# Expert weights of up and down in 1 MB halves, with neighbouring rows in one partition

## The chip, the cores and the metric

The kernel runs on one core of a Trainium2 chip. The metric is the device time of one execution in microseconds (us). The kernel before takes 813.57 us (median of three runs, 813.0 to 815.25).

## The reference

One encoder layer over two sequences, 512 and 256 tokens of width 1024, all in float32: LayerNorm, two attention groups on one input projection, an output projection, LayerNorm, and a mixture of 16 experts (each token goes to the two best of one group of four), then a last LayerNorm. The part that matters here is the mixture:

```python
h = jax.nn.silu(xt @ w_gate[e]) * (xt @ w_up[e])
y = y + gates[:, e:e + 1] * (h @ w_down[e])
```

`w_gate[e]` and `w_up[e]` are 1024 x 512, `w_down[e]` is 512 x 1024; each is 2 MB, so an expert is 6 MB.

## The kernel before

The first 460 us or so (LayerNorm, projections, attention, router) are left as they are. After that the mixture works through tiles: a tile is up to 128 token rows of one expert. The 16 experts need 17 tiles here, and each tile loads its 6 MB of weights anew. The loop is written by hand for each engine; each engine runs its own list in order, and semaphores tie the lists together.

**SP** issues the weight loads (function `load`, L2076 to L2081). Each matrix X (G for gate, U for up, D for down) of a tile comes as four units of 512 KB into the buffers `raw[X][0..3]`, one tile deep: unit i of tile t is issued when the units i of the tile before have been used up (semaphore `s_lo[X]`). In one turn of the loop SP goes through U of the next tile, G of the tile after it, D of the next tile.

**ACT** and **DVE** split each unit for a matmul in two parts: ACT rounds it to `wh_[X][i]` (L2229), after it has landed (`s_raw[X][i]`), and DVE stores the rest, `wl_[X][i]` (L2300). Only when DVE is done with it is the `raw` buffer free.

**POOL** gathers the 128 token rows of the next tile into `xg` with an indirect DMA, and adds the finished rows of a tile to DRAM with another.

**PE** turns the gathered rows (`turn_x`, L2128: eight 128 x 128 transposes of `xg`), multiplies by gate and up (L2143 to L2145, three matmuls for each of eight chunks), turns the hidden rows (`turn_h`, L2152: four transposes of `hid`) and multiplies by down (L2164 to L2166). In a transpose the piece of `xg` or `hid` is the stationary operand: PE loads it with a weight load (PEld in the profile), and the identity streams past.

Which rows of a weight lie in one partition decides which columns of `xg` a chunk takes. A unit of G or U holds 256 rows, two neighbouring rows (4 KB) in each partition, so chunk c takes every second column of `xg`. A unit of D holds 128 rows, one in each partition, so chunk c takes 128 neighbouring columns of `hid`.

Of the kernel before, what the change touches and what calls it, by code (L numbers as in the profile page):

```python
# [27 lines left out]
P = 128  # L28
# [17 lines left out]
FF = 512  # L46
# [14 lines left out]
def encoder_trunk(nc, x_prompt, x_sample, ln0_g, ln0_b, w_in, g_q, g_kv, w_uq, w_ukv, lam_q1, lam_k1,  # L61
# [34 lines left out]
    ident = small("ident", [P, P])  # L96
# [286 lines left out]
    ax = [at(f"ax{i}", (38, 198)[i], [P, D]) for i in range(2)]  # L383
    x1T = at("x1T", 202, [P, KD, P])

    raw = {X: [at(f"raw{X}{i}", 78 + 16 * n + 4 * i, [P, 2 * FF]) for i in range(4)] for n, X in enumerate("GUD")}

    raw_g2 = [at(f"rawG2{i}", (70, 194, 198, 202)[i], [P, 2 * FF]) for i in range(4)]

# [87 lines left out]
    s_lo = {X: sem(f"e{X}_low") for X in "GUD"}  # L477
    s_raw = {X: [sem(f"raw{X}{i}_landed") for i in range(4)] for X in "GUD"}

    def unit_src(X, e, i):  # L480

        if X == "D":
            return w_down[0, bass.ds(e, 1), i * P:(i + 1) * P, :].rearrange("a p n -> p (a n)")
        w = w_gate if X == "G" else w_up
        return w[0, bass.ds(e, 1), 2 * i * P:(2 * i + 2) * P, :].rearrange("a (p c) n -> p (a c n)", c=2)

    def unit_dst(X, i, t=0):
        return raw_of(X, t, i)[:]
# [1155 lines left out]
    with nc.Block() as block:  # L1644

        @block.sync
        def _(sp):
            front_sync(sp)
            sp.wait_ge(s_pv, 3 * NT)
            for i in range(3):  # L1650
                sp.dma_start(unit_dst("G", i), unit_src("G", 0, i)).then_inc(s_raw["G"][i], 16)
            sp.wait_ge(s_o, 12)
            sp.dma_start(ln1g_sb[:], bcast(ln1_g[0], D)).then_inc(s_ln1w, 16)
            sp.dma_start(ln1b_sb[:], bcast(ln1_b[0], D)).then_inc(s_ln1w, 16)
            sp.wait_ge(s_pv, DT)
            sp.dma_start(wr_sb[:], w_router.rearrange("(c p) n -> p c n", p=P)).then_inc(s_rt, 16)
            sp.dma_start(br_sb[:], bcast(b_router, NE)).then_inc(s_rt, 16)
            for X in "UD":
                for i in range(4):
                    sp.dma_start(unit_dst(X, i), unit_src(X, 0, i)).then_inc(s_raw[X][i], 16)  # L1660
            sp.wait_ge(s_zrow, 1)
            sp.dma_start(x1_rows[TOK:TOK + 1, :], ax[1][0:1, :]).then_inc(s_zst, 16)
            sp.dma_start(acc_rows[TOK:TOK + 1, :], ax[1][0:1, :]).then_inc(s_zst, 16)
            for t in range(NT):
                if t == NT - 1:
                    sp.wait_ge(s_o, 24)
                    sp.dma_start(unit_dst("G", 3), unit_src("G", 0, 3)).then_inc(s_raw["G"][3], 16)
                sp.wait_ge(s_x1, t + 1)
                sp.dma_start(x1_rows[t * P:(t + 1) * P, :], res[:, t, :]).then_inc(s_x1st, 16)
                sp.wait_ge(s_ax, t + 1)  # L1670
                sp.dma_start(acc_rows[t * P:(t + 1) * P, :], ax[t % 2][:]).then_inc(s_stored[t % 2], 16)
            sp.wait_ge(s_zst, 32)
            for i in range(2):
                sp.wait_ge(s_stored[i], 16 * (NT // 2))
            sp.wait_ge(s_x1st, 16 * NT)

            for i in range(4):
                sp.wait_ge(s_lo["G"], i + 1)
                sp.dma_start(unit_dst("G", i), unit_src("G", 1, i)).then_inc(s_raw["G"][i], 16)


            sp.wait_ge(s_o, 24)
            sp.wait_ge(s_log, NT)
            for i in range(4):
                sp.wait_ge(s_raw["G"][i], 32)
                sp.dma_start(unit_dst("G", i, 2), unit_src("G", 2, i)).then_inc(s_raw["G"][i], 16)

        @block.tensor
        def _(pe):
# [60 lines left out]
        @block.scalar  # L1750
        def _(act):
            front_act(act)

            def high0(X, units):

                for i in units:
                    act.wait_ge(s_raw[X][i], 16)
# [314 lines left out]
    with nc.Block() as block:  # L2072

        @block.sync
        def _(sp):
            def load(X, t):  # L2076
                e = sp.value_load(tile_expert[0:1, bass.ds(t, 1)], min_val=0, max_val=NE - 1)
                for i in range(4):

                    sp.wait_ge(s_lo[X], 4 * t + i - 3)  # L2080
                    sp.dma_start(unit_dst(X, i), unit_src(X, e, i)).then_inc(s_raw[X][i], 16)  # L2081


            for X in "UD":
                for i in range(4):
                    sp.wait_ge(s_lo[X], i + 1)
                    sp.dma_start(unit_dst(X, i), unit_src(X, 1, i)).then_inc(s_raw[X][i], 16)
            load("U", 2)
            for i in range(4):

                sp.wait_ge(s_raw["G"][i], 48)
                sp.wait_ge(s_lo["G"], 4 + i + 1)
                sp.dma_start(unit_dst("G", i), unit_src("G", 3, i)).then_inc(s_raw["G"][i], 16)
# [12 lines left out]
            sp.wait_ge(s_scatter, 16 * count - 16)  # L2106
            for t in range(NT):
                sp.dma_start(res[:, t, :], acc_rows[t * P:(t + 1) * P, :]).then_inc(s_acc[t], 16)
            for t in range(NT):
                sp.wait_ge(s_yr, t + 1)  # L2110
                dst = y_prompt[0, t * P:(t + 1) * P, :] if t < NT_P else y_sample[0, (t - NT_P) * P:(t - NT_P + 1) * P, :]
                sp.dma_start(dst, res[:, t, :]).then_inc(s_out, 16)
            sp.wait_ge(s_out, 16 * NT)

        @block.tensor
        def _(pe):
            def xg_chunk(c):

                return xg[:].rearrange("p (i m j) -> p i j m", i=4, j=2)[:, c // 2, c % 2, :]

            def turn_x(t):

# [8 lines left out]
            def inner(X, t, units):  # L2131

                out = psum["GU".index(X)][:]
                for i in units:
# [10 lines left out]
                        last = nc.tensor.matmul(out, xgT_h[:, c, :], wl_[X][i][:, cs], start=False, stop=(c == KD - 1))  # L2145
                    last.then_inc(s_used[X], 1)

            def turn_h(t):
                wait(pe, s_hid, t + 1)
                wait(pe, s_hl, t)  # L2150
                for j in range(4):
                    last = nc.tensor.transpose(psum[6][:, j * P:(j + 1) * P], hid[:, j * P:(j + 1) * P], ident[:])  # L2152
                last.then_inc(s_ht, 1)

            def down(t):
# [67 lines left out]
        def _(act):  # L2223
            def high(X, t, units=range(4)):
                for i in units:
                    wait(act, s_raw[X][i], 16 * t + 16)

                    wait(act, s_used[X], used0[X] + 4 * t + i - 3)
                    nc.scalar.activation(wh_[X][i][:], raw_of(X, t, i)[:], ACT.Copy).then_inc(s_hi[X], 1)  # L2229
# [266 lines left out]
```

## Time and profile before

| what | value |
|---|---|
| median of the runs | 813.57 us |
| profiled execution | 813.27 us |
| its span, first to last instruction | 811.5 us |
| PE busy | 736.1 us (91%) |
| DVE busy | 584.5 us (72%) |
| ACT busy | 482.3 us (59%) |
| share of the chain that ended last: PE, DMA | 18%, 15% |

The shares are means over the whole span; the mixture, from about 464 us on, has its own limits and is read from its own stretch. A time in a row below counts from the start of the span. "granted clock" or PEclk is the clock that TensorE was granted, as a share of 2.4 GHz. The chain of waits follows the work that ended last back from the end of the program.

### The profile page before, as it was taken

To read this page: it belongs to the slowest core of one execution; us is meant where nothing else is said; L and a number is where in the kernel's file an instruction comes from. 1 tells how busy PE (TensorE), PEld (TensorE's weight loads), DVE (VectorE), ACT (ScalarE), POOL (GpSimd) and SP (SyncE) were. 2 spreads that over 40 slices of the span, in tenths; PEclk is the share of its full clock that TensorE was granted. 3 is DMA by queue.
4 is the path that set the end of the run, shared out by engine and by line. 5 is a ranking of instruction groups with operands and counts; after the bars stand their busy time and mean duration, and the time that the engine had idled before them with its cause. 6 is when DMAs were issued, how large, how long until landed. Compare 5 with 4: busy or idle time off the path is not lost. (4 is left out here: it accounts for less than half of the span.)

```text
span 811.5 us, 12644 instructions
## 1 busy us (share of the span) xinstructions
PE 736.1 (91%) x3799; PEld 607.6 (75%) x3799; DVE 584.5 (72%) x975; ACT 482.3 (59%) x874; POOL 265.6 (33%) x293
## 2 busy tenths in 40 slices
PE   3999989998899789999998299999999999999985
PEld 3898878877788577767787177888887777777862
DVE  6974355555545676777675879999988888888757
ACT  3344345555544656676035347888878778888635
POOL 3133266655654233334421024222222222222111
PEclk9999999999999969999996589999999999999998
DMA  9724220222025673212734649999999999999763
GB/s 342 250 87 149 98 78 2 79 65 65 2 65 179 211 308 117 70 49 78 290 124 174 241 138 363 384 375 390 396 379 385 376 375 365 388 384 375 284 207 155
DMA packets 71484, 179.35 MB, mean 221 GB/s; under 512 B 11687, under 2 KB 28071, under 8 KB 71444
## 3 DMA queue, kind: packets, MB, share of 16 engines
q1 hardware_dynamic: 66692, 166.34, 54.4%
q0 software_dynamic: 4752, 12.51, 6.2%
q8 instruction: 22, 0.36, 0.2%
q14 instruction: 18, 0.15, 0.1%
HBM read 153.20 MB, written 30.42 MB: 226 GB/s over the span
## 5 line engine op out<-in xcount | busy, mean ns | idle before, releaser
L2300 DVE TENSOR_TENSOR eDl<-rawD,eDh 128x1024 fp32r<-128x1024 f32 x68 | 80.3, 1221 | 12.0 <-ACT eDh L2229 11.8
L1265 POOL TENSOR_SCALAR me<-me,mrec 128x512 f32<-128x512 f32 (+1 forms) x48 | 64.9, 1354 | 55.4 <-DVE mrec L1444 55.4
L2300 DVE TENSOR_TENSOR eUl<-rawU,eUh 128x1024 fp32r<-128x1024 f32 x68 | 78.8, 1220 | 4.5 <-ACT eUh L2229 2.3
L2300 DVE TENSOR_TENSOR eGl<-rawG,eGh 128x1024 fp32r<-128x1024 f32 x64 | 75.6, 1221 | 7.0 <-ACT eGh L2229 6.7
L2424 POOL DMA_INDIRECT acc_rows<-yg,idx_s x16 | 29.7, 1859 | 134.1 <-ACT yg L2254 134.1
L2229 ACT ACTIVATE eGh<-rawG 128x1024 fp32r<-128x1024 f32 x64 | 65.5, 1058 | 6.9 <-DMA rawG<-in_w_gate 5.8
L1071 ACT ACTIVATE pT_h<-bank 128x512 fp32r<-128x512 f32 (+1 forms) x48 | 25.2, 526 | 73.9 <-PE bank L781 73.9
L1450 DVE TENSOR_TENSOR pT_l<-bank,pT_h 128x512 fp32r<-128x512 f32 (+1 forms) x48 | 28.9, 602 | 50.2 <-ACT pT_h L1071 50.2
L2229 ACT ACTIVATE eDh<-rawD 128x1024 fp32r<-128x1024 f32 x64 | 64.0, 1056 | 0.0
L2143 PE MATMUL bank<-eGh,xgT_h 128*128 128x512 f32 x136 | 56.8, 417 | 7.6 <-DVE xgT_l L2305 6.5
L2229 ACT ACTIVATE eUh<-rawU 128x1024 fp32r<-128x1024 f32 x64 | 62.7, 1052 | 0.0
L2143 PE MATMUL bank<-eUh,xgT_h 128*128 128x512 f32 x136 | 54.6, 401 | 0.0
L2145 PE MATMUL bank<-eGl,xgT_h 128*128 128x512 f32 x136 | 54.1, 398 | 0.0
L2144 PE MATMUL bank<-eGh,xgT_l 128*128 128x512 f32 x136 | 53.8, 395 | 0.0
L2145 PE MATMUL bank<-eUl,xgT_h 128*128 128x512 f32 x136 | 53.2, 391 | 0.0
L2144 PE MATMUL bank<-eUh,xgT_l 128*128 128x512 f32 x136 | 52.9, 389 | 0.0
L2166 PE MATMUL bank<-eDl,hT_h 128*128 128x512 f32 x128 | 49.9, 390 | 0.0
L2164 PE MATMUL bank<-eDh,hT_h 128*128 128x512 f32 x128 | 49.8, 389 | 0.0
L2165 PE MATMUL bank<-eDh,hT_l 128*128 128x512 f32 x128 | 49.8, 389 | 0.0
L646 PE MATMUL bank<-xT_h,wb_h 128*128 128x256 f32 (+1 forms) x128 | 44.9, 351 | 3.9 <-DVE q_raw L1431 2.4
L646 PE MATMUL bank<-xT_h,wb_l 128*128 128x256 f32 (+1 forms) x128 | 43.8, 342 | 0.0
L2235 ACT ACTIVATE xgT_h<-bank 128x512 fp32r<-128x512 f32 x34 | 20.3, 596 | 39.5 <-PE bank L2145 26.9
(343 smaller groups left out, 2184.7 us busy)
## 6 DMA issues: line engine op xcount, KB each, us to landing
rawG<-in_w_gate SPq DMA_DIRECT2D x68, 512.0 KB, 14.9
rawU<-in_w_up SPq DMA_DIRECT2D x68, 512.0 KB, 11.7
rawD<-in_w_down SPq DMA_DIRECT2D x68, 512.0 KB, 13.1
wb_raw<-in_w_in SPq DMA_DIRECT2D x8, 512.0 KB, 4.7
wo_raw<-in_w_o SPq DMA_DIRECT2D x8, 512.0 KB, 7.5
xln_rows<-res SPq DMA_DIRECT2D x6, 512.0 KB, 3.9
dqk_high<-st_h SPq DMA_DIRECT2D x8, 384.0 KB, 2.3
dqk_low<-st_l SPq DMA_DIRECT2D x8, 384.0 KB, 3.3
```

The source lines that it names most:

```text
L646: last = nc.tensor.matmul(out, pairs[i][0], pairs[i][1], start=(i == 0), stop=(i == n - 1))
L1265: nc.gpsimd.tensor_scalar(e, e, mrec[:, g % NSB:g % NSB + 1], None, ALU.mult).then_inc(m_p, 1)
L1450: nc.vector.tensor_tensor(pT_l[x][:, :, qs], psum[2 + g % 2][:, 0:n].rearrange("p (j q) -> p j q", q=P), f32(pT_h[x][:, :, qs]), ALU.subtr ...
L2143: nc.tensor.matmul(out, xgT_h[:, c, :], wh_[X][i][:, cs], start=(c == 0), stop=False)
L2144: nc.tensor.matmul(out, xgT_l[:, c, :], wh_[X][i][:, cs], start=False, stop=False)
L2145: last = nc.tensor.matmul(out, xgT_h[:, c, :], wl_[X][i][:, cs], start=False, stop=(c == KD - 1))
L2164: nc.tensor.matmul(out, hT_h[:, cs], wh_["D"][c][:, ns], start=(c == 0), stop=False)
L2165: nc.tensor.matmul(out, hT_l[:, cs], wh_["D"][c][:, ns], start=False, stop=False)
L2166: last = nc.tensor.matmul(out, hT_h[:, cs], wl_["D"][c][:, ns], start=False, stop=(c == 3))
L2229: nc.scalar.activation(wh_[X][i][:], raw_of(X, t, i)[:], ACT.Copy).then_inc(s_hi[X], 1)
L2300: nc.vector.tensor_tensor(wl_[X][i][:], raw_of(X, t, i)[:], f32(wh_[X][i][:]), ALU.subtract).then_inc(s_lo[X], 1)
L2424: pool.indirect_dma_start(out=acc_rows, out_offset=bass.IndirectOffsetOnAxis(ap=idx_s[:, 0:1], axis=0), in_=yg[:], in_offset=None, bounds_ ...
```

## The change

The units of U and D are loaded in pairs. A pair is one DMA of 1 MB: 512 rows of U with four neighbouring rows (8 KB) in each partition, or 256 rows of D with two neighbouring rows (8 KB). The buffers of a pair are one tile; the four `raw` units are views into it, so that ACT and DVE work on the same units as before. G stays in units of 512 KB, but its rows take the same order as those of U: of the four rows that belong to a partition, unit 0 takes the first two and unit 1 the last two, so that it reads 4 KB out of every 8 KB. The chunks follow: chunk c of `xg` takes every fourth column (before every second), chunk c of `hid` every second (before neighbouring ones).

```diff
+    raw_pair = {X: [at(f"pair{X}{h}", 78 + 16 * n + 8 * h, [P, 4 * FF]) for h in range(2)] for n, X in enumerate("GUD") if n}
+    raw = {X: [raw_pair[X][i // 2][:, i % 2 * 2 * FF:(i % 2 + 1) * 2 * FF] for i in range(4)] for X in "UD"}
...
+    def pair_src(X, e, h):
         if X == "D":
-            return w_down[0, bass.ds(e, 1), i * P:(i + 1) * P, :].rearrange("a p n -> p (a n)")
+            return w_down[0, bass.ds(e, 1), 2 * h * P:(2 * h + 2) * P, :].rearrange("a (p c) n -> p (a c n)", c=2)
+        return w_up[0, bass.ds(e, 1), 4 * h * P:(4 * h + 4) * P, :].rearrange("a (p c) n -> p (a c n)", c=4)
+    def gate_src(e, i):
+        rows = w_gate[0, bass.ds(e, 1), 4 * (i // 2) * P:(4 * (i // 2) + 4) * P, :].rearrange("a (p c) n -> p a c n", c=4)
+        return rows[:, :, 2 * (i % 2):2 * (i % 2) + 2, :].rearrange("p a c n -> p (a c n)")
+    def landed(X, i):
+        return s_raw[X][i if X == "G" else i // 2]
...
-                for i in range(4):
+                for i in range(4) if X == "G" else (1, 3):
                     sp.wait_ge(s_lo[X], 4 * t + i - 3)
-                    sp.dma_start(unit_dst(X, i), unit_src(X, e, i)).then_inc(s_raw[X][i], 16)
+                    if X == "G":
+                        sp.dma_start(unit_dst(X, i), gate_src(e, i)).then_inc(s_raw[X][i], 16)
+                    else:
+                        sp.dma_start(raw_pair[X][i // 2][:], pair_src(X, e, i // 2)).then_inc(s_raw[X][i // 2], 16)
...
             def xg_chunk(c):
-                return xg[:].rearrange("p (i m j) -> p i j m", i=4, j=2)[:, c // 2, c % 2, :]
+                return xg[:].rearrange("p (h m k) -> p h k m", h=2, k=4)[:, c // 4, c % 4, :]
...
+            def hid_chunk(c):
+                return hid[:].rearrange("p (h m k) -> p h k m", h=2, k=2)[:, c // 2, c % 2, :]
...
-                    last = nc.tensor.transpose(psum[6][:, j * P:(j + 1) * P], hid[:, j * P:(j + 1) * P], ident[:])
+                    last = nc.tensor.transpose(psum[6][:, j * P:(j + 1) * P], hid_chunk(j), ident[:])
...
             def high(X, t, units=range(4)):
                 for i in units:
-                    wait(act, s_raw[X][i], 16 * t + 16)
+                    wait(act, landed(X, i), 16 * t + 16)
```

On SP the loads of U in the loop stand like this in the kernel before. An ISA row with a wait stands for the wait of the DMA behind it; `eU_low` counts the units of U that DVE has finished.

```order
L2080 REGISTER_ALU
L2081 ISA [waits eU_low]
L2081 DMA rawU0_203<-in_w_up 128x1024
L2080 REGISTER_ALU
L2081 ISA [waits eU_low]
L2081 DMA rawU1_204<-in_w_up 128x1024
L2080 REGISTER_ALU
L2081 ISA [waits eU_low]
L2081 DMA rawU2_205<-in_w_up 128x1024
L2081 ISA [waits eU_low]
L2081 DMA rawU3_206<-in_w_up 128x1024
```

And the same place after the change:

```order
L2089 REGISTER_ALU
L2093 ISA [waits eU_low]
L2093 DMA pairU0_199<-in_w_up 128x2048
L2093 ISA [waits eU_low]
L2093 DMA pairU1_200<-in_w_up 128x2048
```

Four loads with four waits became two loads with two waits, each for the second unit of its pair. D changes in the same way, and G keeps its four loads.

On ACT the rounding of U in the first turn of the loop stands like this before (`rawU0_landed` is the semaphore of the load of unit 0):

```order
L2229 ACTIVATE eUh0_215<-rawU0_203 128x1024 [waits eU_used,rawU0_landed]
L2229 ACTIVATE eUh1_216<-rawU1_204 128x1024 [waits eU_used,rawU1_landed]
L2229 ACTIVATE eUh2_217<-rawU2_205 128x1024 [waits eU_used,rawU2_landed]
L2229 ACTIVATE eUh3_218<-rawU3_206 128x1024 [waits eU_used,rawU3_landed]
L2241 ACTIVATE gsil_6322<-bank0 128x512 [waits hidden,eG_used]
```

And after the change:

```order
L2245 ACTIVATE eUh0_211<-pairU0_199 128x1024 [waits eU_used,rawU0_landed]
L2245 ACTIVATE eUh1_212<-pairU0_199 128x1024 [waits eU_used,rawU0_landed]
L2245 ACTIVATE eUh2_213<-pairU1_200 128x1024 [waits eU_used,rawU1_landed]
L2245 ACTIVATE eUh3_214<-pairU1_200 128x1024 [waits eU_used,rawU1_landed]
L2257 ACTIVATE gsil_6314<-bank0 128x512 [waits hidden,eG_used]
```

The first unit of a pair now waits for the whole pair. No instruction of PE, DVE or POOL moves; PE's twelve transposes for each tile read their stationary operand at another step.

## Rows read from the trace of the kernel before

**Rows 1.** Busy time of each engine by stretch, with granted clock and DMA share.

```profile
core 0: us, PE busy (x) PEld busy (x) DVE busy (x) ACT busy (x) POOL busy (x), PEclk, DMA share, GB/s
480.00:500.00 20.00, 18.95 (x89) 15.29 (x87) 19.30 (x22) 12.91 (x16) 6.83 (x5) 1.00 0.72 249
560.00:580.00 20.00, 20.00 (x95) 16.71 (x94) 18.44 (x19) 17.00 (x22) 5.22 (x6) 1.00 1.03 393
660.00:680.00 20.00, 19.30 (x90) 15.73 (x89) 17.72 (x17) 16.37 (x21) 4.93 (x5) 1.00 1.01 375
```

**Rows 2.** Chain of waits, transposes on it: start us, us, what.

```profile
474.57 0.95 PE bank L2128 x8
...
513.03 1.22 PE bank L2128 x8
...
540.27 0.44 PE bank L2152 x4
...
548.90 0.95 PE bank L2128 x8
...
566.71 0.94 PE bank L2128 x8
...
751.81 0.94 PE bank L2128 x8
```

**Rows 3.** Chain of waits, 605 to 734 us.

```profile
605.05 16.07 DMA rawG<-in_w_gate
...
642.38 16.31 DMA rawG<-in_w_gate
658.71 1.07 ACT eGh L2229
659.81 1.24 DVE eGl L2300
661.19 16.26 DMA rawG<-in_w_gate
...
717.54 16.30 DMA rawG<-in_w_gate
```

**Rows 4.** Weight loads of transposes, both lines, 530 to 590 us (ns min/median/max).

```profile
L2128 PEld LDWEIGHTS bank<-ident,xg x32: 195/209/209, 530.7 to 585.0; 128*128 128x128 f32 x32
...
L2152 PEld LDWEIGHTS bank<-ident,hid x12: 138/139/140, 539.9 to 575.9; 128*128 128x128 f32 x12
```

**Rows 5.** Weight loads of transposes at half clock, and those stretches' clock.

```profile
L1700 PEld LDWEIGHTS bank<-ident,res x11: 224/230/370, 433.8 to 440.3; 128*128 128x128 f32 x11
...
L2128 PEld LDWEIGHTS bank<-ident,xg x8: 197/226/226, 464.3 to 465.6; 128*128 128x128 f32 x8
...
434.00:441.00 7.00, 6.25 (x29) 5.45 (x27) 3.50 (x3) 5.59 (x8) 0.00 (x0) 0.50 0.76 246
...
464.00:466.60 2.60, 1.96 (x8) 1.58 (x8) 1.79 (x2) 0.92 (x2) 0.18 (x1) 0.50 0.08 28
```

**Rows 6.** DMA of 605 to 735 us, then of 93 to 102 us.

```profile
DMA packets 14023, 49.35 MB, mean 380 GB/s; under 512 B 1976, under 2 KB 1976, under 8 KB 14023
q1 hardware_dynamic: 12007, 43.71, 85.3%
...
q1 hardware_dynamic: 1328, 1.31, 45.4%
```

**Rows 7.** Loads that open the stream, and what frees their buffers.

```profile
484.95 4.53 SPq L2087 DMA_DIRECT2D rawD<-in_w_down  x4
...
489.04 4.62 DVE L2300 TENSOR_TENSOR eUl<-rawU,eUh 128x1024 fp32r<-128x1024 f32 x4
```

**Rows 8.** A gather's issue on POOL, its reader on PE, gathers' median to landing.

```profile
646.51 1.06 POOL L497 DMA_INDIRECT xg<-x_rows,idx_g  x1 [1.02 <-issue]
...
657.70 1.11 PE L2128 MATMUL bank<-ident,xg 128*128 128x128 f32 x8
...
xg<-x_rows,idx_g POOLq DMA_INDIRECT x7, 8.1
```

More of the change, by code:

```diff
@@ L384, in encoder_trunk @@
     x1T = at("x1T", 202, [P, KD, P])
-    raw = {X: [at(f"raw{X}{i}", 78 + 16 * n + 4 * i, [P, 2 * FF]) for i in range(4)] for n, X in enumerate("GUD")}
+    raw_pair = {X: [at(f"pair{X}{h}", 78 + 16 * n + 8 * h, [P, 4 * FF]) for h in range(2)] for n, X in enumerate("GUD") if n}
+    raw = {X: [raw_pair[X][i // 2][:, i % 2 * 2 * FF:(i % 2 + 1) * 2 * FF] for i in range(4)] for X in "UD"}
+    raw["G"] = [at(f"rawG{i}", 78 + 4 * i, [P, 2 * FF]) for i in range(4)]
     raw_g2 = [at(f"rawG2{i}", (70, 194, 198, 202)[i], [P, 2 * FF]) for i in range(4)]
@@ L478, in encoder_trunk @@
     s_raw = {X: [sem(f"raw{X}{i}_landed") for i in range(4)] for X in "GUD"}
-    def unit_src(X, e, i):
+    def pair_src(X, e, h):
         if X == "D":
-            return w_down[0, bass.ds(e, 1), i * P:(i + 1) * P, :].rearrange("a p n -> p (a n)")
-        w = w_gate if X == "G" else w_up
-        return w[0, bass.ds(e, 1), 2 * i * P:(2 * i + 2) * P, :].rearrange("a (p c) n -> p (a c n)", c=2)
+            return w_down[0, bass.ds(e, 1), 2 * h * P:(2 * h + 2) * P, :].rearrange("a (p c) n -> p (a c n)", c=2)
[5 more added lines that the diff above has]
+        return s_raw[X][i if X == "G" else i // 2]
     def unit_dst(X, i, t=0):
@@ L1650, in _ @@
             for i in range(3):
-                sp.dma_start(unit_dst("G", i), unit_src("G", 0, i)).then_inc(s_raw["G"][i], 16)
+                sp.dma_start(unit_dst("G", i), gate_src(0, i)).then_inc(s_raw["G"][i], 16)
             sp.wait_ge(s_o, 12)
@@ L1658, in _ @@
             for X in "UD":
-                for i in range(4):
-                    sp.dma_start(unit_dst(X, i), unit_src(X, 0, i)).then_inc(s_raw[X][i], 16)
+                for h in range(2):
+                    sp.dma_start(raw_pair[X][h][:], pair_src(X, 0, h)).then_inc(s_raw[X][h], 16)
             sp.wait_ge(s_zrow, 1)
@@ L1666, in _ @@
                     sp.wait_ge(s_o, 24)
-                    sp.dma_start(unit_dst("G", 3), unit_src("G", 0, 3)).then_inc(s_raw["G"][3], 16)
+                    sp.dma_start(unit_dst("G", 3), gate_src(0, 3)).then_inc(s_raw["G"][3], 16)
                 sp.wait_ge(s_x1, t + 1)
@@ L1678, in _ @@
                 sp.wait_ge(s_lo["G"], i + 1)
-                sp.dma_start(unit_dst("G", i), unit_src("G", 1, i)).then_inc(s_raw["G"][i], 16)
+                sp.dma_start(unit_dst("G", i), gate_src(1, i)).then_inc(s_raw["G"][i], 16)
             sp.wait_ge(s_o, 24)
@@ L1685, in _ @@
                 sp.wait_ge(s_raw["G"][i], 32)
-                sp.dma_start(unit_dst("G", i, 2), unit_src("G", 2, i)).then_inc(s_raw["G"][i], 16)
+                sp.dma_start(unit_dst("G", i, 2), gate_src(2, i)).then_inc(s_raw["G"][i], 16)
         @block.tensor
@@ L1756, in high0 @@
                 for i in units:
-                    act.wait_ge(s_raw[X][i], 16)
+                    act.wait_ge(landed(X, i), 16)
                     nc.scalar.activation(wh_[X][i][:], raw[X][i][:], ACT.Copy).then_inc(s_hi[X], 1)
@@ L2077, in load @@
                 e = sp.value_load(tile_expert[0:1, bass.ds(t, 1)], min_val=0, max_val=NE - 1)
-                for i in range(4):
+                for i in range(4) if X == "G" else (1, 3):
                     sp.wait_ge(s_lo[X], 4 * t + i - 3)
-                    sp.dma_start(unit_dst(X, i), unit_src(X, e, i)).then_inc(s_raw[X][i], 16)
+                    if X == "G":
+                        sp.dma_start(unit_dst(X, i), gate_src(e, i)).then_inc(s_raw[X][i], 16)
+                    else:
+                        sp.dma_start(raw_pair[X][i // 2][:], pair_src(X, e, i // 2)).then_inc(s_raw[X][i // 2], 16)
             for X in "UD":
-                for i in range(4):
-                    sp.wait_ge(s_lo[X], i + 1)
-                    sp.dma_start(unit_dst(X, i), unit_src(X, 1, i)).then_inc(s_raw[X][i], 16)
+                for h in range(2):
+                    sp.wait_ge(s_lo[X], 2 * h + 2)
+                    sp.dma_start(raw_pair[X][h][:], pair_src(X, 1, h)).then_inc(s_raw[X][h], 16)
             load("U", 2)
@@ L2092, in _ @@
                 sp.wait_ge(s_lo["G"], 4 + i + 1)
-                sp.dma_start(unit_dst("G", i), unit_src("G", 3, i)).then_inc(s_raw["G"][i], 16)
+                sp.dma_start(unit_dst("G", i), gate_src(3, i)).then_inc(s_raw["G"][i], 16)
             load("D", 2)
```

## The prediction

> **What bounds the kernel now.** I read the busy time by stretch first, to see which engine is full where. In the mixture TensorE has its full granted clock; from 500 us on PE is busy in 19.3 to 20 of 20 us, and the sixteen DMA engines have a share of 1.01 to 1.03, so both are full [rows 1]. The chain of waits says which of the two sets the pace. Up to about 600 us it runs along PE: turn_x comes at 548.90 and at 566.71 us, so a tile takes 17.80 us [rows 2]. From 605 us on it runs along the loads of gate: a load of 16.3 us, the rounding on ACT (1.07), the rest on DVE (1.24), and the next load; at 642.38, 661.19 and, three turns later, 717.54 us, so a tile takes 18.8 us there [rows 3]. A load lasts that long because it queues behind the others: the DMA engines are full. So there are two limits close together, PE at 17.80 us for a tile and DMA at about 18.8, and DMA began with a lead that it has used up at 605 us. From turn_x of tile 3 (513.03 us) to that of tile 16 (751.81 us) [rows 2] there are 13 tiles in 238.8 us; at PE's pace they would take 231.4. DMA costs 7.4 us in all, and that is the most that a cheaper DMA can give back.
>
> **The change, part by part.** *Transposes on PE.* No instruction is added, but the eight pieces of xg are read at a step of four words instead of two, and the four pieces of hid at two instead of one. The trace has both smaller steps. At a step of one a weight load takes 139 ns, at a step of two 209 ns [rows 4]. On the chain four transposes of hid take 0.44 us, 0.110 each, and eight of xg take 0.95 us, 0.119 each [rows 2]: the longer load is all but covered by the stream of the identity. Is it the reading that takes longer? At half clock (0.50 granted, 1.2 GHz) the step of one takes 230 ns and the step of two 226 [rows 5]. So the load at step one follows PE's clock (139 against 230), and that at step two hardly does (209 against 226): it is held up by fetching the words, not by PE. A load that is held up by its fetches is no longer covered when they double again.
>
> The price of step four stands in no row, so I bound it. Below: a word that is not next to the one before costs one fetch, however far away it is; then step four is like step two, and costs nothing. Less than nothing is excluded, since the same 1,024 words of a partition are read. Above: the load grows by 70 ns for each doubling's worth of fetches, 139, 209, then 209 + 140 = 349 ns, and none of it overlaps: 0.349 - 0.119 = 0.23 us for each transpose, 1.84 for a tile. Between them: the pace of 0.119 is the fetching itself, and doubles, 0.238 us, or 0.119 x 8 = 0.95 us for a tile. I take this one, because it is the step that the nearest row has just made (from a load hidden under 0.110 to one that shows at 0.119), carried on once. hid goes to step two, whose price is known: (0.119 - 0.110) x 4 = 0.04. PE's tile becomes 17.80 + 0.95 + 0.04 = 18.79 us.
>
> The Trainium skill (Advanced Engine Details and Errata, SBUF Cachelines) says that SBUF has lines of 16 bytes, that two reads of one line are enough to hide the memory's latency, and that a new line for each read costs. By that rule step two (two words of a line) would be free, and the trace does not agree (139 against 209 ns); step four (one word of a line) would pay, which speaks for this forecast and against the lower bound, but the rule gives no size.
>
> *Fewer and larger DMAs.* What does a packet cost beside its bytes? Two stretches give two equations, engine time = a x packets + b x MB. In 605 to 735 us 12,007 packets and 43.71 MB take 0.853 x 16 x 130 = 1,774 us; in 93 to 102 us, with small packets, 1,328 packets and 1.31 MB take 0.454 x 16 x 9 = 65.4 us [rows 6]. That gives a = 0.0126 us and b = 37.1 us for a MB, or 0.165 us for 4 KB. The 43.71 MB are 10,671 packets of 4 KB; the other 1,336 are 16 for each of 83 transfers. So on each engine U and D are 8 x (8 + 1) = 72 packets for a tile. If the rows of 8 KB go as one packet, 4 x (8 + 1) = 36 are left, 36 x 0.0126 = 0.45 us less; if they are cut at 4 KB, 68 are left, 0.05 less. No row shows which: in the first stretch every packet is under 8 KB. I take 0.45 as likelier, since the count fits one packet for each row as long as it is. DMA's tile becomes 18.3 or 18.75 us: under PE's 18.79 either way. That is why DMA falls out of the forecast: PE never gets ahead of it.
>
> The Trainium skill (DMA: Bandwidth & Descriptors, Rules for kernel authors) asks for 1 MB or more in a DMA for full bandwidth. By its fixed cost of about 2 us for each DMA, four DMAs fewer would give up to 8 us for a tile, an estimate; but here a load of 512 KB waits behind a dozen others (16.3 us, of which its own bytes take 1.3) and the engines are full [rows 1, 3], so this trace does not agree that the fixed cost is on the path.
>
> *Coarser waits.* A pair is issued when its second unit is free, 1.15 us after the first (four units of U in 4.62 us on DVE), and the stream of loads that starts at 484.95 us starts that much later [rows 7]. The first unit of a pair lands with the second, up to 8 x 0.165 = 1.3 us later. Together that takes up to 2.5 us from DMA's lead, once. Behind the waiting load SP has only later loads, and G frees its buffers after U. While PE sets the pace the lead is not used, so I count nothing; without that cover it costs 2.5 us.
>
> *Gate in pieces of 4 KB out of 8 KB.* The same bytes in the same number of packets; rows show no price. I take none; if it cost as much for G as 8 KB packets save for U and D, DMA would be at 18.8 to 19.2, 0 to 5 us over the 13 tiles.
>
> *Gathers* share the engines with larger packets: 8 packets on each engine could each wait 0.15 us longer, 1.2 us. The gather issued at 646.51 us takes about 8 us (8.1 is the median of its kind), and its turn_x starts at 657.70 [rows 8], so 3 us cover it.
>
> **The sum**, against the profiled execution of 813.27 us: 13 tiles at 18.79 are 244.3 us in place of 238.8, +5.5. Outside them, turn_x of tiles 1 and 16 stands on the chain as well (474.57 and 751.81 us [rows 2]), +1.9; turn_x of tile 0 runs at half clock, where the stream covers more, and a few turn_h add 0.1 to 0.2. Together +7.6, 820.9 us. The median shown is 0.3 us over that execution: 821.0.
>
> **Rivals.** *Step four is free and 8 KB rows are one packet.* DMA gives back 13 x 0.45 = 5.9 us and loses 2.5 of its lead: 813.3 - 3.4 + 0.2 for hid = 810.0, faster. For it: the small difference on the chain between steps one and two (0.009). Against: the loads of 209 ns, which do not follow the clock.
> *Step four is free and packets stay at 4 KB.* 13 x 0.05 = 0.7 us back, 2.5 lost: 815.2. For it: that every packet now is at most 4 KB.
> *Step four costs half of what I take,* 0.06 us for each transpose: PE's tile is 18.32, 13 of them 238.2 (-0.6), and +1.1 outside: 813.8 with large packets, 816.2 with small ones, where DMA is late again.
> *Loads no longer overlap at all,* 0.349 us: a tile of 19.68, +17 us on the 13 and +3.8 outside, 834. Against: loads of 209 ns already run at a pace of 119.
>
> **How the numbers follow.** Forecast 0.48 (its own range 818.5 to 823.5); half price 0.16; free with large packets 0.20; free with small ones 0.11; no overlap 0.05. A measurement here can tell 0.3% from no change, so faster is under 811.1 and slower over 816.0. Faster: three quarters of the third case and a little of others, 0.17. Same: the rest of it, most of the half price and of the fourth, 0.27. Slower 0.56. The range, 810.0 to 823.5, leaves out half of the third case, the last, and a tail: about 0.18.
>
> **What would show it.** Right: eight transposes of xg on the chain at about 1.9 us instead of 0.95 (0.24 a piece), weight loads of xg well over 209 ns and of hid at 209, tiles of 18.8 us from start to end, and no stretch in which the chain runs along loads of gate. The packet count of the same stretch tells 8 KB from 4 KB. Wrong: transposes of xg still at 0.95 us; or a chain that runs along loads of U or D, whose first unit now waits for the second; or loads of gate that are longer than 16.3 us although PE is the slower one.

## The result, and the profile after

The changed kernel takes 818.23 us, median of 22 runs (815.31 to 822.3), against 815.29 for the kernel before in the same session (22 runs, 812.58 to 818.72). The ratio is 1.0035, with an interval of 1.0019 to 1.0051: slower, by 2.9 us. The profiled execution takes 816.17 us, its span 814.4 against 811.5.

The forecast had the sign, a size that was more than twice too large (7.6 us), and the wrong place, so that the sign came true by luck. First the place that it named, the transposes on PE. The chain of waits of the changed kernel, transposes on it (start us, us, what; L2140 turns xg, L2168 turns hid):

```profile
534.87 0.96 PE bank L2140 x8
...
544.05 0.47 PE bank L2168 x4
...
552.73 0.96 PE bank L2140 x8
...
570.59 0.96 PE bank L2140 x8
...
588.45 0.96 PE bank L2140 x8
```

Eight transposes of xg take 0.96 us where they took 0.95, and hid 0.47 instead of 0.44; a tile in which PE sets the pace takes 17.86 us where it took 17.80 [rows 2]. The weight loads of the same stretch as before [rows 4] (ns min/median/max):

```profile
L2140 PEld LDWEIGHTS bank<-ident,xg x32: 197/211/213, 534.5 to 589.0; 128*128 128x128 f32 x32
...
L2168 PEld LDWEIGHTS bank<-ident,hid x12: 196/202/210, 543.7 to 579.8; 128*128 128x128 f32 x12
```

A step of four words loads in 211 ns, a step of two in 209 before; hid at a step of two now takes 202 instead of 139, and on the chain that shows as 0.03 us for four transposes.

So the time must come from elsewhere. The step from tile to tile shows where it is first lost. The chain about the gather of tile 3 and the products behind its transposes, then the same transposes in PE's order of time (in brackets: idle before, and what ended it), then busy times by stretch (columns as in [rows 1]):

```profile
503.63 11.48 DMA xg<-x_rows,idx_g
...
515.24 1.97 PE bank L2140 x8
517.22 0.43 PE bank L2155
...
518.50 0.40 PE bank L2155
```

```profile
515.24 1.97 PE L2140 MATMUL bank<-ident,xg 128*128 128x128 f32 x8 [1.93 <-DMA xg<-x_rows,idx_g]
```

```profile
500.00:515.00 15.00, 12.26 (x55) 9.54 (x53) 13.90 (x15) 12.34 (x16) 6.07 (x5) 1.00 1.03 374
515.00:519.00 4.00, 3.76 (x14) 3.33 (x15) 3.26 (x3) 1.85 (x2) 2.49 (x2) 0.57 1.01 412
519.00:540.00 21.00, 21.00 (x99) 17.58 (x98) 16.52 (x17) 15.40 (x19) 4.70 (x5) 1.00 0.95 352
```

The gather takes 11.48 us. In the kernel before, the same pieces of the chain and of PE's order read

```profile
503.25 9.66 DMA xg<-x_rows,idx_g
...
513.03 1.22 PE bank L2128 x8
...
531.11 0.94 PE bank L2128 x8
```

```profile
513.03 1.22 PE L2128 MATMUL bank<-ident,xg 128*128 128x128 f32 x8 [0.18 <-DMA xg<-x_rows,idx_g]
```

PE waits 1.93 us for the gather where it waited 0.18, and then has a granted clock of 0.57 over 515 to 519 us (for most of it the 1.2 GHz level, after the wait). The next tile's transposes start at 534.87 instead of 531.11. The weight loads, whose buffers come free later behind a late PE, then fill the DMA engines less: a share of 0.95 in 519 to 540 us, where the kernel before has 1.03.

Later the loads set the pace again. A turn, in what follows, is the time from one issue of a buffer's load to its next issue, one tile later. The chain from 611 us on, with one whole turn:

```profile
611.46 15.15 DMA pairD<-in_w_down
...
626.71 1.07 ACT eDh L2245
...
627.81 1.01 DVE eDl L2316
...
628.95 1.23 DVE eDl L2316
...
630.34 14.89 DMA pairD<-in_w_down
...
743.55 14.65 DMA pairD<-in_w_down
```

It ran along gate [rows 3]; now it runs along down. Between landing and next issue a pair has two units to round, 3.7 us (626.61 to 630.34), where a unit of gate had 2.5 (658.69 to 661.19 [rows 3]). From 611.46 to 743.55 us seven turns take 18.87 us each; before it was 18.75 (605.05 to 717.54, six turns [rows 3]). The DMA of 605 to 735 us:

```profile
DMA packets 10021, 49.46 MB, mean 380 GB/s; under 512 B 1528, under 2 KB 1528, under 8 KB 6441
...
q1 hardware_dynamic: 8005, 43.82, 85.3%
```

In q1 there are 4,002 packets fewer than in [rows 6], and 10,021 - 6,441 = 3,580 packets are now of 8 KB, where there was none: a row is one packet. The share and the GB/s are unchanged, the bytes nearly so.

One number compares the mixtures of all kernels without the few us by which single executions reach it sooner or later: the time from the first silu on ACT (there is one for each tile) to the last. Kernel before, then the changed one:

```profile
L2241 ACT ACTIVATE gsil<-bank x17: 573/581/597, 474.6 to 766.1; 128x512 f32<-128x512 f32 x17
```

```profile
L2257 ACT ACTIVATE gsil<-bank x17: 580/587/599, 475.0 to 770.3; 128x512 f32<-128x512 f32 x17
```

291.5 against 295.3 us, +3.8. Of this 3.4 are there when tile 4 is turned (531.11 - 474.6 = 56.5; 534.87 - 475.0 = 59.9). The same rows split the 3.4: tile 3 is turned 1.8 us later (513.03 - 474.6 = 38.4; 515.24 - 475.0 = 40.2), which is the longer wait, and the other 1.6 come between tile 3 and tile 4, where PE no longer waits but has its transposes at 1.97 instead of 1.22 us and four products at 0.40 to 0.43 instead of 0.23, at the lower clock. The changed execution begins the mixture 0.4 us later and takes 1.3 us less behind it (814.4 - 770.3 against 811.5 - 766.1), so that the spans differ by 2.9.

### The profile page after: what moved, and what is told of

The parts are those of the page before. It is cut to its first block and busy times, and to the rows that moved or that the text cites. A ratio compares the mean times of both kernels' runs of the same rounds, so it can differ in the third digit from the quotient of the medians.

```text
span 814.4 us, 12428 instructions
## 1 busy us (share of the span) xinstructions
PE 738.6 (91%) x3799; PEld 611.5 (75%) x3799; DVE 583.3 (72%) x975; ACT 481.8 (59%) x874; POOL 262.3 (32%) x293
## 5 line engine op out<-in xcount | busy, mean ns | idle before, releaser
L2316 DVE TENSOR_TENSOR eDl<-pairD,eDh 128x1024 fp32r<-128x1024 f32 x68 | 80.3, 1221 | 14.3 <-ACT eDh L2245 14.0
L2316 DVE TENSOR_TENSOR eUl<-pairU,eUh 128x1024 fp32r<-128x1024 f32 x68 | 78.8, 1220 | 4.3 <-ACT eUh L2245 2.3
L2245 ACT ACTIVATE eDh<-pairD 128x1024 fp32r<-128x1024 f32 x64 | 64.1, 1056 | 2.5 <-DMA pairD<-in_w_down 2.5
L2245 ACT ACTIVATE eUh<-pairU 128x1024 fp32r<-128x1024 f32 x64 | 62.3, 1050 | 0.0
```

Source lines behind the costliest of these rows:

```text
L2316: nc.vector.tensor_tensor(wl_[X][i][:], raw_of(X, t, i)[:], f32(wh_[X][i][:]), ALU.subtract).then_inc(s_lo[X], 1)
```

## The experiments

Each was timed beside the kernel before, and its ratio is to that kernel in the same session. "Length" is the time from first to last silu in the one profiled execution. The kernel before and the two that leave its loads as they are (the steps alone, the gather issued earlier) have lengths of 291.5, 291.7 and 291.8. Kernels with pairs agree less well: turns of the same loads come out at 18.66 to 18.87 us below, and no run shows why, so that over nine such turns a length there is good to a us or two. Three theories stood behind the first runs on the place of the loss (those on pairs with 4 KB rows, on gate, and on the gather): A, larger packets hold up the gather of tile 3; B, a pair waits for two units and lands as one; C, gate read in 4 KB out of every 8 is slower.

**The steps alone** settle the forecast's own term. The kernel before, with two lines changed:

```diff
-                return xg[:].rearrange("p (i m j) -> p i j m", i=4, j=2)[:, c // 2, c % 2, :]
+                return xg[:].rearrange("p (h m k) -> p h k m", h=2, k=4)[:, c // 4, c % 4, :]
...
-                    last = nc.tensor.transpose(psum[6][:, j * P:(j + 1) * P], hid[:, j * P:(j + 1) * P], ident[:])
+                    last = nc.tensor.transpose(psum[6][:, j * P:(j + 1) * P], hid[:].rearrange("p (h m k) -> p h k m", h=2, k=2)[:, j // 2, j % 2, :], ident[:])
```

> The kernel before, with nothing changed but the steps at which PE's transposes read: xg at a step of four words instead of two, hid at two instead of one (the loads keep their row order, so the product pairs the wrong rows). The forecast's term (0.95 us for xg and 0.04 for hid in every tile): a tile of 18.79 us, 821 us. Step four free: eight transposes of xg at 0.95 us, a tile of 17.80 to 17.86 us, and the time of the kernel before within 1 us. Half price: 815 to 817 us.

815.27 us against 814.87, ratio 0.9998 (0.9983 to 1.0012). Its chain, transposes of xg:

```profile
532.35 0.96 PE bank L2128 x8
...
550.21 0.96 PE bank L2128 x8
```

17.86 us from one to the next, and eight transposes still take 0.96 us. The 0.95 us of the forecast is not there: step four costs 0.01 us for a tile, hid 0.03.

**Pairs with rows of 4 KB.** One DMA of 1 MB for two units, but rows, order and steps of before. Against the changed kernel, the source of a pair:

```diff
         if X == "D":
-            return w_down[0, bass.ds(e, 1), 2 * h * P:(2 * h + 2) * P, :].rearrange("a (p c) n -> p (a c n)", c=2)
-        return w_up[0, bass.ds(e, 1), 4 * h * P:(4 * h + 4) * P, :].rearrange("a (p c) n -> p (a c n)", c=4)
+            return w_down[0, bass.ds(e, 1), 2 * h * P:(2 * h + 2) * P, :].rearrange("a (j p) n -> p (a j) n", j=2)
+        return w_up[0, bass.ds(e, 1), 4 * h * P:(4 * h + 4) * P, :].rearrange("a (j p c) n -> p (a j) (c n)", j=2, c=2)
...
```

> The pairs of U and D as one DMA of 1 MB each with the waits of the change, but with the row order of the kernel before: every packet is 4 KB again, PE reads xg at step two and hid at step one, gate is as before. Only the coarser waits and the smaller number of DMAs are left of the change. Theory A (larger packets hold up the gather of tile 3, PE waits longer and loses its clock, and that is the 2.9 us): about the time of the kernel before, ratio 0.999 to 1.001, gather of tile 3 on the chain at about 9.7 us. Theory B (a pair waits for two units and lands as one, which costs DMA's lead of 2.5 us): +1.8 to +3 us, ratio 1.002 to 1.004. Theory C (gate read in 4 KB out of every 8 KB is slower and eats what large packets save): about the time before.

817.78 us, ratio 1.0033 (1.0010 to 1.0056), length 296.3 (474.1 to 770.4). The pairs alone, without one packet of 8 KB, cost as much as the whole change. But the place is another: the gather of tile 3 takes 10.04 us, PE waits 0.56 us for it and keeps its clock (1.00 in 500 to 520 us), and the loss builds up in the turns. Chain, first and last of seven turns, and DMA of 605 to 735 us:

```profile
609.89 15.27 DMA pairD<-in_w_down
...
743.56 14.76 DMA pairD<-in_w_down
```

```profile
DMA packets 13370, 48.57 MB, mean 374 GB/s; under 512 B 1515, under 2 KB 1515, under 8 KB 13370
```

19.10 us for a turn instead of 18.75, and 374 GB/s instead of 380. What was priced at 2.5 us once costs 0.35 us in every turn in which the loads set the pace. That the wait for the second unit is what costs it is only argued: a pair is also one DMA in place of two and lands as one, and no run takes these apart. SP's waits for DVE to free a buffer, in 605 to 735 us, do grow, though fewer loads wait; the kernel before and the changed one (us in total, times, longest):

```profile
SPq L2081 <- DVE eDl L2300: 35.6, 28, 3.5
SPq L2081 <- DVE eUl L2300: 20.5, 28, 1.3
```

```profile
SPq L2093 <- DVE eDl L2316: 45.0, 14, 5.2
SPq L2093 <- DVE eUl L2316: 27.1, 14, 2.5
```

Against these 19.10 us stand 18.87 in the changed kernel, with rows of 8 KB: the large packets are worth something after all.

**Gate units without gaps.** Gate is read as before, in whole rows of 4 KB side by side, so that the product pairs other rows than the reference's. Against the changed kernel:

```diff
-        rows = w_gate[0, bass.ds(e, 1), 4 * (i // 2) * P:(4 * (i // 2) + 4) * P, :].rearrange("a (p c) n -> p a c n", c=4)
-        return rows[:, :, 2 * (i % 2):2 * (i % 2) + 2, :].rearrange("p a c n -> p (a c n)")
+        return w_gate[0, bass.ds(e, 1), 2 * i * P:(2 * i + 2) * P, :].rearrange("a (p c) n -> p (a c n)", c=2)
```

> The changed kernel with one part undone: a unit of gate reads its 256 rows without gaps, as before (its rows then stand in another order than the chunks of xg, so that the product with gate is another one). Theory C: the DMA-bound turns fall from 18.87 us to about 18.4, 2 to 5 us faster than the changed kernel, ratio to the kernel before 0.997 to 1.001. Theories A and B: as the changed kernel, ratio 1.003 to 1.005, turns of 18.8 to 18.9 us.

819.11 us, 1.0034 (1.0010 to 1.0059). Nothing comes back: theory C falls. Length 294.7. Its turns take 18.66 us (613.24 to 743.86, seven); the changed kernel with the gather issued earlier (next), with the gaps, has 18.67, so the gaps are not what separates these from 18.87.

**The gather earlier**, on the changed kernel and on the one before: POOL issues the gather of tile t+2 ahead of the scatter of tile t-1 (the DMA that adds finished rows to DRAM), not after it.

```diff
             def add_rows(t):
-                wait(pool, s_yg, t)
-                nc.gpsimd.tensor_copy(gate_col[:], gate_tab[:, bass.ds(t, 1)]).then_inc(s_gcol, 1)
...
             def iteration(t, last):
+                wait(pool, s_yg, t - 1)
+                nc.gpsimd.tensor_copy(gate_col[:], gate_tab[:, bass.ds(t - 1, 1)]).then_inc(s_gcol, 1)
                 if not last:
-                    gather(t + 1)
+                    gather(t + 2)
                 add_rows(t - 1)
...
+            gather(2)
```

> The changed kernel, with the gathers of POOL one tile earlier in its list: the gather of tile t+2 stands ahead of the adding of tile t-1, right after the copy of the gate column. The gather of tile 3 then starts when turn_x of tile 2 is done (about 495 us) instead of 503.6. Theory A: PE no longer waits at 503 to 515 us and keeps its clock; turn_x of tile 3 starts some 6 us earlier, the gain is cut by the DMA-bound turns that follow: 1.5 to 4 us faster than the changed kernel, ratio to the kernel before 0.998 to 1.001. Theory B: the DMA-bound turns decide the end, so at most 1 us faster than the changed kernel, ratio 1.002 to 1.004.

> The kernel before with the same earlier gathers and nothing else. It tells whether the wait at 503 to 513 us is on the path there as well. Theory A: PE starts tile 3 some 6 us earlier, and DMA is late that much earlier: between 0 and 4 us faster than the kernel before, ratio 0.995 to 1.000, less than what the same edit gives the changed kernel. Theory B: no difference between what the edit gives here and there.

On the changed kernel 814.97 us, 1.0001 (0.9978 to 1.0023); on the kernel before 815.13, 1.0001 (0.9980 to 1.0022). The changed kernel gets back about 2.8 us and the other nothing; the 2.8 is 1.0035 less 1.0001, of two sessions, each known to 1.3 to 1.8 us. Silu of the first:

```profile
L2257 ACT ACTIVATE gsil<-bank x17: 586/586/599, 479.4 to 771.7; 128x512 f32<-128x512 f32 x17
```

292.3 us, 3.0 less than without the edit. PE's clock is full in 500 to 520 us, and the turns take 18.67 us (595.87 to 726.54, seven). Not all of the 3.0 comes from the place of tile 3. The ninth silu, by which the loads have taken over in both, comes 144.0 us after the first (623.42) and without the edit 145.3 (620.28): 1.3 us are there, and the other 1.7 come from the shorter turns, for which no run gives a reason.

The edit also does a second thing: it puts the scatter later. At tile 3 ACT then waits 1.76 us for the scatter to have read yg (with down's pairs alone, shown below, 1.99), and PE 1.14 us behind ACT; the changed kernel without the edit has neither wait.

**Without a third of PE's work**: one of the three products of each chunk is dropped in three kernels (the "light" ones), so that the loads set the pace sooner and more often.

```diff
-                        nc.tensor.matmul(out, xgT_l[:, c, :], wh_[X][i][:, cs], start=False, stop=False)
-                        last = nc.tensor.matmul(out, xgT_h[:, c, :], wl_[X][i][:, cs], start=False, stop=(c == KD - 1))
+                        last = nc.tensor.matmul(out, xgT_l[:, c, :], wh_[X][i][:, cs], start=False, stop=(c == KD - 1))
...
```

> The kernel before, with the third product of every chunk left out in the mixture's gate, up and down (the low part of the weights times the high part of the rows; the output lacks it). PE's tile falls from 17.80 by 24 products of 0.23 us to about 12.3 us, so that nothing but the loads can set the pace from the first tile on; the loads themselves, their buffers and their waits are as before. Theory Q (the bytes set the pace of the full DMA engines): a tile takes 18.8 us along loads of gate from tile 3 on. If PE's lead had mattered, the time falls by up to 7 us; if the loads were the limit from 500 us on, it stays within 2 us of the kernel before.

> The changed kernel with the same third products left out (the output lacks them): what the 8 KB rows are worth where nothing but loads sets the pace. Theory P (a packet costs 0.0126 us beside its bytes, as the prediction had it): 36 packets fewer on each engine, a tile of 18.35 us against 18.8 in the light kernel before, 13 tiles give back 5.9 us, less 2.5 for the pairs: 3.4 us faster than the light kernel before. Theory Q (only bytes count on full engines): the same 18.8 us, and the pairs' later issue shows, 1 to 2.5 us slower than the light kernel before.

> The first experiment (pairs in one DMA of 1 MB, but rows of 4 KB in the order of before) with the same third products left out (the output lacks them). Theory P: 4 packets fewer on each engine for a tile, 18.75 us, so 3.4 + 2 = about 5 us slower than the light changed kernel. Theory Q: the same time as the light changed kernel within 1 us, and 1 to 2.5 us over the light kernel before, once and not for each tile.

811.61 us (0.9961, 0.9941 to 0.9981), 814.28 (0.9995, 0.9975 to 1.0015) and 816.24 (1.0012, 0.9992 to 1.0031). A third of the mixture's products less gives 3.3 us, and the profile has them behind the last silu. Silu of the light kernel before, then of the light changed kernel:

```profile
L2239 ACT ACTIVATE gsil<-bank x17: 581/584/597, 475.6 to 768.7; 128x512 f32<-128x512 f32 x17
```

```profile
L2255 ACT ACTIVATE gsil<-bank x17: 581/586/597, 472.8 to 769.5; 128x512 f32<-128x512 f32 x17
```

The light kernel before has a length of 293.1, not less than 291.5 with all products; what is shorter is the time behind the last silu (810.3 - 768.7 = 41.6 against 45.4; the other kernels with all products have 43.7 to 45.5 there). So between first and last silu dropping the products gained nothing. PE is not wholly out of the way, though: its granted clock is 0.87 in 540 to 600 us, and in the light kernel before a load of gate stands on the chain only every second turn, with ACT, DVE and PE between.

The change still costs 2.7 us here and the 4 KB pairs 4.6. In length the change costs 296.7 - 293.1 = 3.6 us. PE waits for the gather of tile 3 in both light kernels (1.70 and 2.25 us), and only 1.2 of the 3.6 us are there when tile 4 is turned (529.67 - 475.6 = 54.1; 528.09 - 472.8 = 55.3). A loss as large as that of the whole change thus arises mostly behind that place. Chains with loads on them, before (two turns between rows), changed (three) and 4 KB pairs (six):

```profile
644.68 15.68 DMA rawG<-in_w_gate
...
682.25 15.69 DMA rawG<-in_w_gate
```

```profile
609.28 15.06 DMA pairD<-in_w_down
...
665.88 15.22 DMA pairD<-in_w_down
```

```profile
608.34 15.50 DMA pairD<-in_w_down
...
722.70 15.67 DMA pairD<-in_w_down
```

18.79, 18.87 and 19.06 us. The 18.35 of theory P (packets cost time beside their bytes) is not seen, but neither is the equality of theory Q (only bytes count): the pairs lengthen a turn by 0.3, and the rows of 8 KB take most of that back.

**One kind of pair at a time**, with all products and light. Up alone: gate in the matching order, down as before. Down alone: up and gate as before. The loop of loads, changed kernel against up alone:

```diff
-                for i in range(4) if X == "G" else (1, 3):
+                for i in (1, 3) if X == "U" else range(4):
...
```

> Only the up weights go in pairs of 1 MB with rows of 8 KB (gate in the matching order, xg read at four words); the down weights stay in four loads of 512 KB, hid at a step of one. Theory W: a pair adds about 1.1 us of rounding between its landing and its next issue, which lengthens the turn only where the buffer has no slack. In the kernel before, a gate load takes 16.25 + 2.5 us of a turn of 18.75 (no slack), down 14.6 + 2.5 (1.7 of slack), up 12.9 + 2.5 (3.4 of slack). By W a pair of up stays hidden, the chain runs along gate, the 8 KB rows save half of 0.23, a turn of 18.65 us, and the time is that of the kernel before or 1 us less (814 to 815.3). Theory V (the loss is the later opening of the stream, which up pairs begin): the loss of 2.5 to 2.9 us is here, 817 to 818.

> Only the down weights go in pairs of 1 MB with rows of 8 KB (hid read at two words); up and gate as before, xg at a step of two. Theory W: the pair uses up the slack of down (14.6 + 3.6 us, and one load that has to wait for two), the chain runs along down, a turn of 18.85 to 19.0 us, and the time is 1.5 to 2.9 us over the kernel before (816.5 to 818). Theory V (the later opening of the stream by up pairs): no loss, the time of the kernel before within 0.7 us.

> The kernel with pairs of up weights alone, without the third product of every chunk of the mixture (the output lacks it), beside the light kernels of before (18.79 us for a turn from 644 us on), of the change (18.85) and of the coarse pairs (19.1). Theory W: chain along gate, a turn of 18.65 us, 811 us or a little less than the light kernel before (811.6). If 8 KB rows save nothing: 18.79 and 811.6. If pairs cost wherever they are: 18.9 to 19.0, 813.

> The kernel with pairs of down weights alone, without the third product of every chunk of the mixture (the output lacks it). Theory W: chain along down, a turn of 18.9 to 19.0 us, 813 to 814.5, near the light changed kernel (814.3). If pairs of down cost nothing: 18.7 to 18.8 and 811 to 811.6.

Up alone 817.66 us, 1.0020 (1.0000 to 1.0041), length 293.4; down alone 816.37, 1.0008 (0.9993 to 1.0024), length 293.2. The light ones 813.01 (0.9956, 0.9939 to 0.9973; seven runs) and 811.82 (0.9961, 0.9938 to 0.9984), about the light kernel before (0.9961): by the ratios one kind of pair alone shows no loss there, and only both together do. Theory W (a pair costs only where its buffer has no slack, so in down) had all of the loss in down, and theory V (the later opening of the stream) all of it in up; the lengths give 1.9 to up and 1.7 to down, and neither theory stands alone. Each part is no larger than what a length is good for, and by the ratios up's loss is barely clear of noise and down's is not. The two lose in different ways. Chain of down alone, then of up alone:

```profile
504.35 11.18 DMA xg<-x_rows,idx_g
515.65 1.22 PE bank L2159 x8
```

```profile
518.68 1.16 PE bank L2159 x8
...
557.22 15.73 DMA rawG<-in_w_gate
...
725.24 16.35 DMA rawG<-in_w_gate
```

With down's pairs the gather of tile 3 takes 11.18 us, nearly as long as in the changed kernel (11.48). With up's pairs it takes 9.4 us, but the chain is on the loads from 557 us (76.8 us after the first silu) and not from 605 (130 us after it): the lead that the loads have over PE is lost early. The turns are 18.77 us for down alone (610.95 to 723.54, six) and 18.67 for up alone (557.22 to 725.24, nine), 18.75 before: a pair of one kind with 8 KB rows does not lengthen them.

**The gather earlier, on the parts.**

> Pairs of 1 MB with 4 KB rows, as in the first experiment (1.0033), and the gather of tile t+2 issued ahead of the scatter, as in the third. Theory G (the early issue gives back what the late gather of tile 3 costs): there that gather took 10.0 us and PE stayed at its full clock, so little comes back: 1.002 to 1.003, about 817, and turns of 19.1 us where loads set the pace. Theory H (the early issue makes up for any pair): 1.000, 815.

> Pairs of up alone with 8 KB rows (1.002 without the early issue), and the gather of tile t+2 issued ahead of the scatter. The gather of tile 3 took 9.4 us in that kernel. Theory G: little comes back, 1.001 to 1.002, 816 to 817. Theory H: 1.000 or a little less, 814.5 to 815.5. It beats both kernels only if its turns stay at 18.7 us and the opening loses nothing: 813 to 814.

> Pairs of down alone with 8 KB rows (1.0008 without the early issue), and the gather of tile t+2 issued ahead of the scatter. The gather of tile 3 took 11.2 us in that kernel and its transposes 1.2. Theory G: 1 to 2 us come back, 0.998 to 0.9995, 814 to 815, the best of all. Theory H: the same. If the early issue only helps where both pairs are there: 1.0008, 816.

4 KB pairs: 818.44 us, 1.0035 (1.0015 to 1.0056), length 296.1, turns of 19.14 (605.65 to 720.46, six). Up alone: 814.85, 1.0013 (0.9998 to 1.0028), length 291.7. Down alone: 815.96, 1.0015 (0.9996 to 1.0033), length 293.9. Theory H (the early issue makes up for any pair) falls: pairs of 4 KB keep their whole loss. But the gain of theory G (it gives back what the late gather costs) on down alone, 1 to 2 us, did not come either, though its gather was nearly as late as that of the changed kernel. ACT and PE of that last run, at tile 3, show why:

```profile
520.69 0.69 ACT L2288 ACTIVATE yg<-bank,gate_col 128x512 f32<-128x512 f32 x1 [1.99 <-DMA acc_rows<-yg,idx_s]
```

```profile
526.05 0.49 PE L2174 MATMUL bank<-eGh,xgT_h 128*128 128x512 f32 x1 [1.39 <-DVE xgT_l L2340]
```

Tile 3 is turned 1.8 us sooner after the first silu, and then ACT waits 1.99 us for the scatter that the edit has put later, is late with xgT_h, and PE waits 1.39 us for what follows from it. The next tile is turned only 0.2 us sooner than without the edit. The wait has moved from the gather to the scatter. The changed kernel with the edit has the same wait, 1.14 us on PE, but had also lost 1.6 us to the lower clock, and that came back: its transposes of tile 3 take 1.12 us in PE's order instead of 1.97. No version beats the kernel before.

## Why the prediction was off, step by step

*What bounds the kernel: right.* PE and the loads lie close together; without a third of PE's products the length is 293.1 us where it was 291.5, and the turns keep their 18.8.

*The step of four words: wrong, and it is the step on which the forecast stood.* "The pace of 0.119 is the fetching itself, and doubles" gave 0.95 us for a tile and, with hid's 0.04, 7.6 in all. Measured: 0.96 us for eight transposes instead of 0.95, loads of 211 ns instead of 209, and 815.27 us with the steps alone, 0.4 over the kernel before. The price that held was that of the lower bound, which was set aside: step four costs what step two costs. Whether its reason holds too (one fetch for each word that is not next to the last) no run shows. That the loads at step two hardly follow the clock [rows 5] was read as a sign of fetches that grow with the step; the rows showed no growth. Since PE's tile stays at 17.86 us, PE does get ahead of the loads, and with that DMA, which the forecast had let fall out, is back in it. The rule that was weighed (the Trainium skill, Advanced Engine Details and Errata, SBUF Cachelines: a new line of 16 bytes for each read costs) spoke for a price at step four, and this case's trace does not agree: 211 against 209 ns.

*8 KB rows: the count was right (36 packets fewer on each engine for a tile, 4,002 fewer in 130 us), and 0.45 us of a turn is at the upper end of what was seen.* Between pairs of 4 KB and of 8 KB rows the turn goes from 19.10 and 19.14 to 18.66, 18.67 and 18.87: 0.2 to 0.5 us, and 0.2 between the light kernels. It is not seen against the kernel before because the next term takes it.

*Coarser waits: mis-sized.* They were counted at nothing under PE's cover and at 2.5 us, once, without it. The second unit to be rounded adds 1.2 us to every pass of a buffer that holds one tile (3.7 against 2.5 us from landing to issue), and where the loads set the pace a turn with pairs is 0.35 us longer, each time. That is about as much as the large packets give back, so that turns end at 18.7 to 18.9, near the 18.75 of before.

*Gathers: the size was about right, the cover was not.* 1.2 us longer was the estimate; the gather of tile 3 takes 1.8 longer, and the median in 605 to 735 us goes from 8.1 [rows 8] to 9.7. The 3 us of cover were read at 646 us, in the steady state. At tile 3 there is none: the transposes of 513.03 us [rows 2] wait for that gather in the kernel before already (0.18 us). In the changed kernel PE waits 1.93 us there, then runs at the lower clock, and in its profile 3.4 of the mixture's 3.8 us are lost in this one place, 1.8 by the wait and 1.6 at the lower clock. The clock fell there in the profiles of the changed kernel and of the one without gaps in gate (0.91 and 0.93 granted in 500 to 520 us), and in no other that has all of PE's work. What decides it no run shows: in the light changed kernel PE waited 2.25 us there and still had its transposes at 1.23 us.

Issuing that gather earlier gave back 3.0 us of length and 2.8 of the median; that is shown. That this place is the cause of the whole 2.9 us is not: only 1.3 of the 3.0 are there when the loads take over, the edit puts the scatter later, and the light kernels lose 2.7 us mostly behind it. What the runs allow is that the pairs leave the loads with less lead, and that the late gather, the lower clock and the longer turns each spend some of it.

*Gate in pieces:* right at nothing, within what these runs can tell.

*The rivals.* "Step four free, large packets" had the mechanism of steps and packets right and came to 810.0, faster, because its loss of lead was paid once, and because it had no late gather. The nearest in size, "packets stay at 4 KB" with 815.2 (+1.9), is near by luck: the packets did become 8 KB. Of the signs named for being wrong two appeared: xg at 0.96 us, and a chain along loads of down.

Open, too, is why up's pairs lose the lead early. Their later issue (1.15 us) and later landing (up to 1.3) add up to 2.45 us at most, which would be room enough for the 1.9 us of length, but no run took one of the two away alone.

## What to carry to other kernels

Where buffers hold one tile and the DMA engines are full, a larger DMA can be paid for in every turn by the work between its landing and its next issue; compare that with what its packets save before merging loads. Look for the cover of a delayed transfer at the first tiles as well as in the steady state, and take a wait that already shows on the chain as no cover at all. A price worked out by carrying a trend on once (139, 209, next?) is a bound and not a value. And when an experiment moves one instruction ahead of another, look at who waits for the one that was moved back.

## What the runs showed of the hardware

- A weight load of 128 x 128 words at a step of four words takes 211 ns, at two 202 to 209, at one 139 (medians, full clock): the price is paid between one and two, and no more is added at four.
- Rows of 8 KB go as one packet each (3,580 packets not under 8 KB, where there was none). On full engines turns with them are 0.2 to 0.5 us shorter than with the same pairs in 4 KB rows; the share of the queue (85.3%) and the rate (380 GB/s) are the same in the kernel before and in the changed one, so they do not show it.
- DMAs of 1 MB instead of 512 KB, with the coarser waits that go with them, are slower here: 19.10 us for a turn against 18.75, and 374 GB/s against 380, with the same packets of 4 KB. The Trainium skill (DMA: Bandwidth & Descriptors, Rules for kernel authors) asks for 1 MB or more for the most bandwidth; with buffers of one tile this trace does not agree.
- A gather on another queue takes longer beside larger transfers and packets: 8.1 us before, 9.0 with 4 KB pairs and 9.7 with 8 KB pairs (medians of seven or so in 605 to 735 us, one profile each).
- After a wait of PE its granted clock was 0.57 over 515 to 519 us, and eight transposes took 1.97 us, where they take 1.22 at the full clock.
